# A two-block transformer forward pass in float32: the opening, the end of the first mixer and the order of products behind two norms are rebuilt

## The reference

```python
def rmsnorm(x, g):
    y = x * lax.rsqrt(jnp.mean(x * x, axis=-1, keepdims=True) + NORM_EPS)
    return y * g
# first mixer ("even"): 8 channel groups of 128 columns
proj = rmsnorm(x, norm_pre) @ w_in                 # 1024 -> 6144
xa, za, xb, gb, gc, zb = split(proj, 6)
ua = centred_dwconv(xa, conv_w) + conv_b
ya = rg_lru(ua, forward) + rg_lru(ua, backward)    # gates = sigmoid(ua @ 128x128), then a scan over tokens
ya = ya * silu(za)
yb = gb * centred_dwconv(gc * xb, sc_w) * silu(zb)
x = x + rmsnorm(concat(ya, yb) @ w_out, norm_post) # 2048 -> 1024
# second mixer ("odd"): gated linear attention
q, k, v, r, lr = split(rmsnorm(x, g) @ w_in)
x = x + rmsnorm(attention(q, k, v, lr) * silu(r) @ w_out, norm_post)
# then, in the second block, FFN 1 of layer 0:
a, b = split(rmsnorm(x, g) @ w_in)                 # 1024 -> 2 x 2816
x = x + 0.5 * (silu(a) * b) @ w_out
```

## Time and profile before

| | us |
|---|---|
| median of 3 runs | 3034.52 (3033.64 to 3037.81) |
| the profiled execution | 3036.39 |
| its span in the trace | 3034.6 |
| PE busy | 2821.4 (93%) |
| POOL busy | 1645.3 (54%) |
| DVE busy | 1317.2 (43%) |
| ACT busy | 694.0 (23%) |
| mean PE clock | 0.963 of full |

### The profile page before, as it was taken

One profiled execution on the slowest core, in us unless ns is written; L12 is line 12 of the kernel. 1 busy time (PEld: TensorE's weight loads), 2 busy tenths in 40 slices (PEclk: granted clock), 3 DMA queues, 4 the chain that ended last, 5 costly groups with the idle time before them and its releaser, 6 DMA issues.

```text
span 3034.6 us, 36240 instructions
## 1 busy us (share of the span) xinstructions
PE 2821.4 (93%) x13146; PEld 2211.6 (73%) x13146; DVE 1317.2 (43%) x1601; ACT 694.0 (23%) x1165; POOL 1645.3 (54%) x966
## 2 busy tenths in 40 slices
PE   6999789956779999997899999999999999999999
PEld 4777566734558888885588888878888866788887
DVE  4777613034454134304564133664133456553142
ACT  2444311043221001006521001131001166421010
POOL 3666454500336656560066656656656678666565
PEclk9999898977889999999999999999999989999999
DMA  4222222200113322330033223233223200133222
GB/s 156 88 93 94 66 90 63 84 7 0 48 59 97 101 90 97 90 92 19 6 93 104 90 91 103 86 123 104 91 91 102 70 15 2 31 95 108 85 92 88
DMA packets 60866, 235.52 MB, mean 78 GB/s; under 512 B 6752, under 2 KB 6752, under 8 KB 60512
## 3 DMA queue, kind: packets, MB, share of 16 engines
q1 hardware_dynamic: 60768, 234.21, 24.4%
HBM read 232.08 MB, written 2.10 MB: 77 GB/s over the span
## 4 chain that ended last, share of the span: by engine, by line
PE 87%; DVE 6%; issue 2%; ACT 2%; DVEq 1%; ACTq 1%; DMA 0%; POOL 0%; POOLq 0%; SPq 0%
PE ps L317 24%; PE ps L319 24%; PE ps L318 24%; PE ps L332 1%; PE ps L334 1%; PE ps L333 1%; PE ps L883 1%; PE ps L920 1%; PE ps L900 1%; PE ps L537 1%; PE ps L724 1%; ACTq L1115 1%; PE ps L620 1%; DVE lo L232 1%; PE ps L627 1%
## 5 line engine op out<-in xcount | busy, mean ns | idle before, releaser
L301 POOL TENSOR_TENSOR w_lo<-ring,w_hi 128x1024 fp32r<-128x1024 f32 (+2 forms) x396 | 1026.5, 2592 | 58.1 <-issue 2.8
L299 POOL CAST w_hi<-ring 128x1024 fp32r<-128x1024 f32 (+2 forms) x396 | 446.8, 1128 | 1119.4 <-PE ps L319 944.2
L317 PE MATMUL ps<-hi,w_hi 128*128 128x512 f32 x2208 | 888.5, 402 | 59.5 <-DVE lo L232 31.0
L319 PE MATMUL ps<-hi,w_lo 128*128 128x512 f32 x2208 | 873.8, 396 | 0.0
L318 PE MATMUL ps<-lo,w_hi 128*128 128x512 f32 x2208 | 872.5, 395 | 0.0
L317 PEld LDWEIGHTS ps<-hi,w_hi 128*128 128x128 f32 x2208 | 417.1, 189 | 172.2 <-issue 51.0
L319 PEld LDWEIGHTS ps<-hi,w_lo 128*128 128x128 f32 x2208 | 418.4, 189 | 102.3
L318 PEld LDWEIGHTS ps<-lo,w_hi 128*128 128x128 f32 x2208 | 418.1, 189 | 98.8 <-issue 3.4
L317 PE MATMUL ps<-hid_hi,w_hi 128*128 128x512 f32 x704 | 274.3, 390 | 0.0
L319 PE MATMUL ps<-hid_hi,w_lo 128*128 128x512 f32 x704 | 274.0, 389 | 0.0
L318 PE MATMUL ps<-hid_lo,w_hi 128*128 128x512 f32 x704 | 274.0, 389 | 0.0
(11 more groups left out here) (291 smaller groups left out, 3145.3 us busy)
## 6 DMA issues: line engine op xcount, KB each, us to landing
ring<-in_ffn_in SPq DMA_DIRECT2D x176, 512.0 KB, 3.6
ring<-in_even_in SPq DMA_DIRECT2D x48, 512.0 KB, 4.1
ring<-in_ffn_out SPq DMA_DIRECT2D x32, 768.0 KB, 4.2
ring<-in_ffn_out SPq DMA_DIRECT2D x32, 640.0 KB, 3.9
ring<-in_even_out SPq DMA_DIRECT2D x16, 512.0 KB, 3.6
ring<-in_odd_qk SPq DMA_DIRECT2D x8, 512.0 KB, 3.6
ring<-in_odd_r SPq DMA_DIRECT2D x8, 512.0 KB, 3.6
ring<-in_odd_v SPq DMA_DIRECT2D x8, 512.0 KB, 3.5
```

The costliest lines, as they stand in the source:

```text
L299: nc.gpsimd.tensor_copy(w_hi[:, j % 2, 0:cols], ring[:, j, 0:cols])
L301: nc.gpsimd.tensor_tensor(w_lo[:, j % 2, 0:cols], ring[:, j, 0:cols], w_hi[:, j % 2, 0:cols].bitcast(F32), ALU.subtract).then_inc(sem["w_r ...
L317: nc.tensor.matmul(bank, w_hi[:, j % 2, w], x_hi[:, k, :], start=(start and k == 0), stop=False)
L319: mm = nc.tensor.matmul(bank, w_lo[:, j % 2, w], x_hi[:, k, :], start=False, stop=(stop and k == kt - 1))
```

## The change

The first normed product of the first mixer (channel 0) is made from unscaled x·g (`plain_hi`, `plain_lo`), its six products are scaled afterwards by DVE in PSUM (`scale_plain`), and DVE makes the scaled `hi`, `lo` for channels 1 to 7 meanwhile (`normed`). x comes in eight transfers, the constants in two (472 columns first, the other 6220 behind the first weights), the first weight slot ahead of x. The loop over channels is peeled at both ends. In the last channel, 14 of the 16 tiles of `y_even` are split before its recurrence, and PE makes five output tiles without the last two input tiles first. The weights of `even_out` are laid out in that order. The odd layer's projections begin with half of v by tokens (four banks for each input tile), the other half comes last; its q, k and r tiles use all 8 banks. The first group of FFN 1 of layer 0 goes input tile by input tile over its four output tiles, and the next group's first pair goes to banks 4 and 6. The squares of these two norms go to bank 5.

```diff
-    ("odd_qk", 8, 8 * P), ("odd_r", 8, 8 * P), ("odd_v", 8, 8 * P), ("odd_out", 8, 8 * P),
+    ("odd_v", 4, 8 * P), ("odd_qk", 8, 8 * P), ("odd_r", 8, 8 * P), ("odd_v2", 4, 8 * P), ("odd_out", 8, 8 * P),
...
+EARLY = 5
+EVEN_K = list(range(DT, 2 * DT - 1)) + list(range(DT - 1)) + [2 * DT - 1, DT - 1]
+EVEN_OUT = ([(m, k) for m in range(EARLY) for k in EVEN_K[:-2]] + [(m, k) for m in range(EARLY) for k in EVEN_K[-2:]]
+            + [(m, k) for m in range(EARLY, DT) for k in EVEN_K])
+EVEN_BANK = [0, 1, 2, 4, 5, 6, 7, 0]
...
-        SQ_BANK, TOKEN_BANK, SUM_BANK = 3, 6, 7
+        TOKEN_BANK, SUM_BANK = 6, 7
+
+        def square_bank(s):
+
+            return ps[:, 5 if s in ("odd_pre", "ffn1_0") else 3, :]
...
-            sp.dma_start(consts[:, :], consts_in).then_inc(sem["const_landed"], 16)
-            sp.dma_start(res[:, :, :], x_in).then_inc(sem["x_landed"], 16)
...
+            sp.dma_start(consts[:, 0:N_FIRST], consts_in[:, 0:N_FIRST]).then_inc(sem["const_landed"], 16)
+            even_weight(0, 0)
+            for k in range(DT):
+                sp.dma_start(res[:, k, :], x_in[:, k, :]).then_inc(x_landed[k], 16)
+                if k == 3:
+                    even_weight(0, 1)
+            even_weight(0, 2)
+            even_weight(0, 3)
+            gate_weight(0, 0)
+            gate_weight(0, 1)
+            sp.dma_start(consts[:, N_FIRST:N_CONSTS], consts_in[:, N_FIRST:N_CONSTS]).then_inc(sem["consts_landed"], 16)
+            for s in range(RING, 12):
+                sp.wait_ge(sem["w_ready"], s + 1)
+                even_weight(0, s)
...
+                x_hi, x_lo = (plain_hi, plain_lo) if c == 0 else (hi, lo)
+                for n in range(6):
+                    s = 6 * jj + n
+                    j = s % RING
+                    pe.wait_ge(sem["even_moved"], 12 * i + (s + 1))
+                    pe.wait_ge(sem["w_ready"], 12 * i + ready("even_in", s + 1))
+                    tile_ready = None
+                    if n == 0 and c == 0:
+                        tile_ready = lambda k: pe.wait_ge(sem["plain_low"], k + 1)
+                    if n == 0 and c == 1:
+                        tile_ready = lambda k: pe.wait_ge(sem["even_low"], k + 1)
+                    product(ps[:, j, :], j, DT, x_hi, x_lo, tile_ready)
+                    if n == 1 and c == 0:
+                        sums_pe(pe, "even_pre")
...
+            pe.wait_ge(sem["even_moved"], RING + 6 * RG_HEADS)
+            for n, (m, k) in enumerate(EVEN_OUT):
+                if m == 3 and k == EVEN_K[0]:
                     pe.wait_ge(sem["gates_read"], 1 + RG_HEADS)
...
+                if n % 8 == 0:
+                    pe.wait_ge(sem["w_ready"], ready("even_out", n // 8 + 1))
+                if m == 0:
+                    pe.wait_ge(sem["y_low"], EVEN_K.index(k) + 1)
+                if m == DT - 1 and k == EVEN_K[0]:
+                    pe.wait_ge(sem["y_moved"], 1)
+                bank = ps[:, EVEN_BANK[m], :]
+                w = slice(n % 8 * P, (n % 8 + 1) * P)
...
+                x_hi = hi[:, k, :] if k < DT else lo[:, k - DT, :]
+                nc.tensor.matmul(bank, w_hi[:, j, w], x_hi, start=(k == EVEN_K[0]), stop=False)
+                nc.tensor.matmul(bank, w_lo[:, j, w], x_hi, start=False, stop=False)
+                mm = nc.tensor.matmul(bank, w_hi[:, j, w], y_lo[:, k, :], start=False, stop=(k == EVEN_K[-1]))
+                if n % 8 == 7:
+                    mm.then_inc(sem["slots_used"], 1)
+                    if k == EVEN_K[-1]:
+                        pe.drain().then_inc(sem["y_done"], 1)
+                elif k == EVEN_K[-1]:
+                    mm.then_inc(sem["y_done"], 1)
             sums_pe(pe, "even_post")
...
+            token_product(pe, "odd_v", 0, 0, x_ready(pe, "odd_pre"))
+            sums_pe(pe, "odd_pre")
+            for n in range(2 * DT):
+                name, m = ("odd_qk", "odd_r")[n // DT], n % DT
+                if n == 2:
+                    sums_read(pe, "odd_pre")
+                if 4 <= n < 8:
+                    pe.wait_ge(sem["v_copied"], n - 3)
+                if n >= 8:
+                    pe.wait_ge(sem["proj_copied"], m + 1)
+                pe.wait_ge(sem["w_ready"], ready(name, m + 1))
+                product(ps[:, (4 + m) % 8, :], m, DT, hi, lo)
             pe.wait_ge(sem["weights_gained"], 1)
...
+            pe.wait_ge(sem["r_moved"], 4)
...
             mm.then_inc(sem["lr_done"], 1)
-            pe.wait_ge(sem["lr_copied"], 1)
-            token_product(pe, "odd_v", 0, 4)
             pe.wait_ge(sem["r_moved"], DT)
-            token_product(pe, "odd_v", 1, 0)
+            token_product(pe, "odd_v2", 0, 0)
...
+                    if half == 0 and ffn == "ffn1_0":
+                        for j in range(RING):
+                            pe.wait_ge(sem["w_ready"], ready(name, j + 1))
+                            for k in (2 * j, 2 * j + 1):
+                                tile_ready(k)
+                                for m in range(RING):
+                                    w = slice((k % 2 * RING + m) * P, (k % 2 * RING + m + 1) * P)
+                                    nc.tensor.matmul(ps[:, m, :], w_hi[:, j % 2, w], hi[:, k, :], start=(k == 0), stop=False)
+                                    nc.tensor.matmul(ps[:, m, :], w_hi[:, j % 2, w], lo[:, k, :], start=False, stop=False)
+                                    mm = nc.tensor.matmul(ps[:, m, :], w_lo[:, j % 2, w], hi[:, k, :], start=False,
+                                                          stop=(k == DT - 1))
+                            mm.then_inc(sem["slots_used"], 1)
+                        sums_pe(pe, ffn)
+                        for j in range(2):
+                            pe.wait_ge(sem["w_ready"], RING + ready(name, j + 1))
+                            product(ps[:, 4 + 2 * j, :], j, DT, hi, lo)
+                        way_in(1, False, 2)
...
+                act.wait_ge(x_landed[k], 16)
+                nc.scalar.activation(plain_hi[:, k, :], res[:, k, :], ACT.Identity, scale=con("g_even_pre")[:, k:k + 1])\
+                    .then_inc(sem["plain_high"], 1)
+                square_act(act, "even_pre", k, res[:, k, :])
+            roots_act(act, "even_pre")
...
+                    if c == 0:
+                        act.wait_ge(sem["plain_scaled"], n + 1)
+                    else:
+                        act.wait_ge(sem["slots_used"], 12 * i + used("even_in", s + 1))
+                    nc.scalar.activation(dst, ps[:, s % RING, :], func).then_inc(sem["even_moved"], 1)
+                    if c == 0 and n in (2, 3):
+                        for k in range(4 * n - 8, 4 * n - 4):
+                            act.wait_ge(sem["even_scaled"], k + 1)
+                            nc.scalar.activation(hi[:, k, :], even_tmp[k % 2], ACT.Copy).then_inc(sem["even_high"], 1)
+                if c == RG_HEADS - 1:
+                    y_highs(DT, 2 * DT - 1)
+                    act.wait_ge(sem["even_channel_done"], 1 + RG_HEADS)
+                    y_highs(0, DT - 1)
...
+                if c == RG_HEADS - 1:
+                    act.wait_ge(sem["yb_done"], 1)
+                    y_highs(2 * DT - 1, 2 * DT)
...
+            decay_terms((17, 15, 13, 11))
+            for k in range(DT):
+                dve.wait_ge(sem["plain_high"], k + 1)
+                V.scalar_tensor_tensor(plain_lo[:, k, :], res[:, k, :], con("g_even_pre")[:, k:k + 1],
+                                       plain_hi[:, k, :].bitcast(F32), ALU.mult, ALU.subtract).then_inc(sem["plain_low"], 1)
                 dve.drain()
-                V.tensor_scalar(lt[:, 4, :], lt[:, 5, :], 1.0 / odd, None, ALU.add)
...
+            decay_terms((9, 7, 5, 3, 1))
...
+                def scale_plain(n):
+                    if c == 0:
+                        dve.wait_ge(sem["slots_used"], used("even_in", n + 1))
+                        bank = ps[:, n % RING, :]
+                        V.tensor_tensor(bank, bank, rinv[:, :], ALU.mult).then_inc(sem["plain_scaled"], 1)
+
+                def even_low(k):
+                    dve.wait_ge(sem["even_high"], k + 1)
+                    V.tensor_tensor(lo[:, k, :], even_tmp[k % 2], hi[:, k, :].bitcast(F32), ALU.subtract)\
+                        .then_inc(sem["even_low"], 1)
+
+                def normed(k0, k1):
+                    for k in range(k0, k1):
+                        dve.drain()
+                        V.scalar_tensor_tensor(even_tmp[k % 2], res[:, k, :], con("g_even_pre")[:, k:k + 1], rinv[:, :],
+                                               ALU.mult, ALU.mult).then_inc(sem["even_scaled"], 1)
+                        dve.drain()
+                        if k > k0:
+                            even_low(k - 1)
+                    even_low(k1 - 1)
+
+                def moved(n):
+                    dve.wait_ge(sem["even_moved"], 12 * i + (6 * jj + n + RING))
+
...
+                scale_plain(0)
+                scale_plain(1)
+                moved(1)
```

(65 more changed lines are left out.)

348 lines of the change are left out of this document (157 added, 191 removed).

## The result

The changed kernel takes 2992.61 us (median of four runs, 2990.41 to 2993.57) against 3034.08 for the kernel before beside it: ratio 0.9857, 95% interval 0.9845 to 0.9869. The spans of the two profiled executions, 3034.6 and 2991.2 us, differ by 43.4.

A forecast was written before the change was run, and what follows sets the result against it. PE was taken to bound the kernel, so only its idle time and slow stretches could be won. Opening 5.4 + mixer end 17.6 + odd projections 10.4 + FFN 1 3.6 = 37.0 us: 3034.5 - 37.0 = 2997.5 us, range 2973 to 3016.

The forecast's parts named there:

- Opening: Start of the first mixer: reordered transfers and an unscaled first product win 5.4 us net, bounds 0 and 24.
- 5.5 us lost: Channel 1 of the first mixer: `ua` comes at 103.6, PE wants it at 98.1, so PE loses 5.5 us.
- 1.0 more: Channel 2 of the first mixer: SP's weights, queued behind channel 0's end, are split at 108.2 against gates ending at 107.2.
- The reading by which eleven transfers pay a fixed cost in turn: Opening: about 2.0 us per DMA paid in turn, last x tile at about 30, winning some 6 us less.
- Mixer end: End of the first mixer: early splits and output tiles fill PE's 17.9 us idle, winning 17.6 us, bounds 14 and 19.5.
- The cover: End of the first mixer: 48.6 us of output tiles hide the remaining chain, ending by 378, needed at 385.8; 8 us spare.
- Odd projections: Odd layer's projections: twelve matmuls per input tile keep PE nearly always busy, winning 10.4 us, bounds 7 and 16.2.
- The sign that I had named: DVE's norm work: line 232's successor takes over 2 us beside POOL; staying at 0.75 us would favour no blocking.
- the rival without blocking: DVE's norm work runs at its idle-POOL pace beside splits: gains sum to 70 us, 2964 us; chance 0.13.
- FFN 1: FFN 1's first group: input tile by input tile wins 8.5 us, less a 4.9 us stall: 3.6, bounds -1 and 10.
- the low clock: Both ramps: the clock stays low, 41.0 us instead of 29.8, so gain 14.6 us, 3020 us; chance 0.09.
- The backlog rival: DVE backlog: opening wins nothing, mixer end's cover fails by a few us; gain 22 us, 3013 us; chance 0.12.

The follow-up runs named there:

- both runs with shortened splits: Changed kernel, POOL splitting only 8 of 1024 columns of four weight slots, for timing alone: in the norm's ramp 2989.85 us, in channel 0 2983.49 us.
- the version with the new order: Changed kernel, DVE in channel 0 making all eight normed tiles and scaling all six banks before the convolution: 2986.41 us.
- the version with both edits: Changed kernel, channel 0's normed tiles and scalings ahead of its convolution, and FFN 1's fifth to eighth tile in banks 4, 6, 5, 7: 2981.52 us.
- the run with the late gate load: Changed kernel, SP loading a channel's gate weights after that channel's first three weights instead of ahead of them: 3001.69 us.

## Why the prediction was right, and which term was off

By its own steps:

1. **Opening: 5.4 forecast, 11.1 measured.** This is the mis-sized term. The gain at channel 1's first product was 14.3, forecast 11.9 (that product ends at 67.9, 2.4 earlier than its 70.3). The "5.5 us lost" before channel 1's gates did not happen: they stand 14.7 ahead. The "1.0 more" in channel 2 was 3.6 (14.7 at the gates of channel 1, 11.1 at those of channel 2), since a low clock followed the wait. Two assumptions were off. The first was the landing of the second slot, 8.7 against 11.42: from 2 to 8 us the queue moved 269 to 307 GB/s, where the forecast had taken up to 428 from the earlier trace rows. (By those slices the 5.5 MB of constants and x have moved by 15.3 and not 15.1, a difference that does not matter here.) With the slot later, `plain_lo` started 4.1 us earlier, and what follows up to the sigmoids 2.4 to 4.8 us earlier. The reading by which eleven transfers pay a fixed cost in turn is out: it had the last x tile at about 30, and ACT works on that tile at 20.58. The second was the 30.0 us from sigmoid to `ua`, taken from a steady channel. Here it was 26.6 (68.77 to 95.36), because SP's queue stood behind `even_channel_done` and POOL had nothing to split for 8.0 us; with the weights issued earlier it is 31.6. I had put that wait down as a cost alone; it also took POOL off DVE's chain, and moving it cost 3.3 us. That DVE's chain of channel 0 has no slack is right: delayed further, it moved channel 1's gates by 11.7 us and channel 2's by 7.9. From channel 2 on all gates of the first mixer stand 11.1 ahead.

2. **Mixer end: 17.6 forecast, 16.8 measured.** Waits of 0.6 and 0.6 us stand where 17.9 stood, 1.1 less than forecast; PEclk reads 1.00 from the gates to the row sums. The cover held. The drains were put at some tenths: PE pauses at four tile borders, 1.6 us in all.

3. **Odd projections: 10.4 forecast, 10.8 measured.** The ramp was forecast at 29.8 us and took 29.6. The mechanism is shown: without the splits 24.7, where I had put 24.0 as PE's bound. Line 1483 waits out POOL's subtraction, 2.75 us, as the earlier trace rows had shown for a small instruction. The sign that I had named failed, though: in the ramp the successor of line 232 stays at 0.75 us, because it never starts beside a split, and its neighbours, also with two SBUF inputs, are blocked instead (lines 1481 and 1483: 1.37, 2.75, 1.38 and 2.70 us, 5.3 more than alone). Read by the word, that sign would have spoken for the rival without blocking. PEclk over the ramp is 0.84 and not near 1.

4. **FFN 1: 3.6 forecast, 3.2 measured.** Stall 4.9 forecast, 4.3 measured. I had priced only the wait; with the clock behind it, it costs 6.7. The ramp made good for that: 27.3 us instead of 29.8, with PEclk 0.93. (The end of the four products before, the base of the forecast 8.5, is 893.1 in the trace and not 894.2.)

The sum of the four is 41.8 by fixed points, less 1.5 in the stretch between them. It was forecast at 37.0. The opening's 5.7 us are the bulk of the miss. That it is no more is in part luck: inside the opening one loss was 5.5 too high and the other 2.6 too low. Another 3.1 us of the profiles' difference arise in later code that the change does not touch. Of the rivals, the one without blocking would have needed ramps of 24 us, the low clock ramps of 41. The backlog rival did not happen, and it was a real danger: 11.2 us more on DVE in channel 0 cost 7.9, more than the two losses that I had put into the sum. The Trainium skill's SBUF — State Buffer (Who interferes with whom) has a DVE instruction with two SBUF inputs and a GpSimd (POOL) instruction that reads SBUF exclude each other, the later one fully blocked until the first ends. The trace agrees (2.75 us beside POOL, 0.69 alone), and both runs with shortened splits do.

## What to carry to other kernels

When work is moved to where another engine was idle, cost each pair of instructions that exclude each other, and look for the opposite too: a queue that is held back may be what keeps a chain undisturbed, so that freeing it makes the kernel slower. Inside one engine's queue, put first what others wait for and let the rest fall into its own waits (5.9 us here for moving four calls). When several accumulators end together, their consumers need as many free banks as the backlog is long; two gave 4.2 us, two more 6.7.

## What was not expected of the hardware

- **A short wait can cost more than itself.** Behind 4.3 us of idling PE's clock read 0.50 for the next ten matmuls, which start every 0.43 us instead of every 0.23, and removing the wait gave 6.7 us. Not every wait does: behind the 1.93 us in channel 2 some eight matmuls are slow (the row 101.05:104.90 above), behind the 1.53 us at the same place in the version with the new order none is:

```profile
96.76:101.00 4.24, 4.24 (x18) 3.49 (x19) 1.87 (x2) 4.16 (x7) 4.06 (x2) 1.00 0.42 134
```

- **The same instructions take 225.5 to 229.0 us.** Between the gated attention's first gate matmul and the row sums ahead of FFN 1 nothing differs between these kernels, yet the fourteen profiled executions spread over 3.5 us, with a granted clock of 0.76 in one and 0.78 in another:

```profile
579.60:808.60 229.00, 148.23 (x628) 102.56 (x628) 101.35 (x177) 72.38 (x117) 42.17 (x32) 0.76 0.07 21
```

```profile
572.30:797.90 225.60, 144.82 (x628) 100.06 (x628) 101.36 (x177) 72.31 (x117) 42.14 (x32) 0.78 0.07 21
```

The first row is the changed kernel, the second the version with both edits. PE is busy 3.4 us longer with the same 628 matmuls. So a gain early on can be given back, or grow, in code that is not touched. What sets the clock there was not tried. The 1.5 us above is this: PE is busy 146.72 us there before and 148.23 after.

- **One POOL instruction is sometimes slow.** In six of the fourteen profiled executions one cast at about 1.9 ms, in the same place of the code, holds PE for 2.0 to 3.7 us; casts of this size take 1.04. Here in the run with the late gate load:

```profile
1907.42 6.53 POOL L312 CAST w_hi<-ring 128x1024 fp32r<-128x1024 f32 x1 [1.96 <-PE ps L349]
```

Behind it PE waits 3.7 us. In the changed kernel's own profile the same instruction took 1.82. What delays it was not tried; it hides effects of this size in a single time.
